# Small experts: V's blocks from the 16th on by indirect loads that leave out unpicked rows, with fewer identity products and moved row sums

## The reference, cut to what matters

```python
def peer_ffn(h, w_query, sub_keys, expert_u, expert_v):      # 256 tokens, D = 1024
    q = (xt @ w_query).reshape(T, 8, 2, 128)
    scores = einsum('thpc,hpnc->thpn', q, sub_keys)          # 8 heads, 2 x 128 keys
    ...                                                      # the 16 best key pairs of each head
    idx = ...                                                # 128 of 16384 experts for each token
    gate = softmax(best_s)
    act = gelu(einsum('cd,ced->ce', x, expert_u[idx]))
    y = einsum('ce,ced->cd', gate * act, expert_v[idx])
```

## Time and profile before

| | us |
|---|---|
| median of 3 runs | 2841.92 |
| lowest and highest run | 2835.9 and 2845.36 |
| the profiled execution, its own time | 2837.32 |
| its span | 2835.4 |
| first and last `back` of the first layer (start) | 1336.47 and 1873.93 |
| the same of the second layer | 2278.58 and 2816.04 |

### The profile page before, as it was taken

One profiled execution on the slowest core, in us unless ns is written; L12 is line 12 of the kernel. 1 busy time (PEld: TensorE's weight loads), 2 busy tenths in 40 slices (PEclk: granted clock), 3 DMA queues, 4 the chain that ended last, 5 costly groups with the idle time before them and its releaser, 6 DMA issues. The chain is left out here.

```text
span 2835.4 us, 45847 instructions
## 1 busy us (share of the span) xinstructions
PE 2671.6 (94%) x18652; PEld 2063.7 (73%) x18652; DVE 1527.5 (54%) x2976; ACT 519.8 (18%) x1030; POOL 612.9 (22%) x657
## 2 busy tenths in 40 slices
PE   8989988999987799889999999999998999999997
PEld 8978856555543687889777766678698977776665
DVE  5786533111100455789555467645467965537774
ACT  4543212000000253222000000014432200000000
POOL 0012100111110000114333344400001443325441
PEclk9999989999999899999999999999999999999999
DMA  7410029999999723689999999954258999999995
GB/s 221 151 48 3 3 104 383 419 418 420 419 420 395 263 65 108 227 293 404 409 409 409 365 409 409 409 195 150 82 190 308 364 407 409 409 370 406 409 409 204
DMA packets 260111, 843.20 MB, mean 297 GB/s; under 512 B 30258, under 2 KB 96306, under 8 KB 234944
## 3 DMA queue, kind: packets, MB, share of 16 engines
q1 hardware_dynamic: 182480, 567.60, 52.0%
q0 software_dynamic: 77424, 272.68, 24.4%
HBM read 881.07 MB, written 11.27 MB: 315 GB/s over the span
## 5 line engine op out<-in xcount | busy, mean ns | idle before, releaser
L166 PE MATMUL psum<-constants 128*128 128x256 f32 x2264 | 539.4, 383 | 21.1 <-DMA token_results<-expert_rows,place 11.2
L2418 PEld LDWEIGHTS psum<-all_gates 128*128 128x128 f32 x4096 | 482.8, 193 | 75.0 <-issue 63.0
L166 PEld LDWEIGHTS psum<-constants 128*128 128x128 f32 x2264 | 425.4, 192 | 138.9 <-issue 80.4
L2418 PE MATMUL psum<-all_gates 128*128 128x128 f32 x4096 | 489.2, 277 | 18.3 <-ACT act L2489 10.1
L2441 PE MATMUL psum<-v_raw,act 128*128 128x512 f32 x1024 | 481.4, 592 | 0.7 <-ACT act L2489 0.7
L2538 POOL DMA_INDIRECT all_gates<-expert_u_rows_dram,all_gates x256 | 255.0, 996 | 1014.5 <-DVE all_gates L2615 552.6
L2661 DVE CUSTOM_DVE_ANT_0 all_gates<-all_gates,psum 128x1024 f32<-128x1024 f32 x256 | 309.2, 1219 | 205.9 <-DMA all_gates<-expert_u_rows_dram,all_gates 203.8
L2670 DVE SCALAR_TENSOR_TENSOR psum<-all_gates,psum 128x1024 f32<-128x1024 f32 x254 | 327.1, 1288 | 145.9 <-DMA all_gates<-expert_v_dram,all_gates 141.3
L2538 POOL DMA_INDIRECT all_gates<-expert_v_dram,all_gates x256 | 253.1, 989 | 326.1 <-DVE psum L2670 197.0
L1741 PE MATMUL psum<-piece_raw,tile_cols 128*64 128x256 f32 x2496 | 287.9, 381 | 17.8 <-DMA piece_raw<-w_up_dram 7.6
L2441 PEld LDWEIGHTS psum<-v_raw,act 128*128 128x128 f32 x1024 | 194.4, 190 | 136.7 <-issue 122.4
(11 more groups left out here) (518 smaller groups left out, 3125.1 us busy)
## 6 DMA issues: line engine op xcount, KB each, us to landing
all_gates<-expert_u_dram SPq DMA_DIRECT2D x256, 512.0 KB
v_raw<-expert_v_dram SPq DMA_DIRECT2D x256, 512.0 KB
piece_raw<-w_gate_dram SPq DMA_DIRECT2D x78, 1024.0 KB, 15.0
piece_raw<-w_up_dram SPq DMA_DIRECT2D x78, 1024.0 KB, 23.4
piece_raw<-w_down_dram SPq DMA_DIRECT2D x78, 1024.0 KB, 20.1
in_raw<-w_in_dram SPq DMA_DIRECT2D x48, 1024.0 KB, 11.1
query_raw<-w_query_dram SPq DMA_DIRECT2D x16, 1024.0 KB, 6.5
w_o<-w_o_dram SPq DMA_DIRECT2D x16, 512.0 KB
```

The costliest lines, as they stand in the source:

```text
L166: nc.tensor.matmul(S["psum"][:, bank, T:].rearrange("p (i n) -> p i n", n=P), ident, ident.unsqueeze(1).to_broadcast([P, 2, P]), start=Tru ...
L2418: last = nc.tensor.matmul(PS[:, bank, 0:P], raw_u[:, n % RAW_U, c * P:(c + 1) * P], h_full[:, c, :], start=(c == 0), stop=(c == KD - 1), s ...
```

## The change

- V's blocks 16 to 127 no longer come from SP but from POOL (`load_wanted`), by indirect loads. DVE's `want` marks, in four parts of 28 blocks at the turns 0 to 3 of the back loop, each row whose gate is zero for all dense tokens; such a row gets an index beyond the bound and keeps what the buffer held. A load waits for its part's marks and for PE's `back(n - 7)`.
- POOL's picks stand in its program behind the V load of the same turn (`picks_after`), no longer in one run.
- `FILL` goes from 4 to 2. The last 56 blocks of U are spread over the first 104 turns (`dense_after`).
- Eight picks move into `select(1)` (`beside`), the last ten picks into the layer norm between its halves (`last_picks`).
- The Gelu of the row sums is taken in two halves, behind the gelu of blocks 86 and 106.

```diff
-    FILL = 4
+    SUMS_AFTER = (EARLY + 14, EARLY + 34)
+    FILL = 2
+    DENSE_SPAN = 104
+    BESIDE_CHOICE = 8
+    LAST_PICKS = 10
+    WHOLE, PARTS = 16, 4
...
+        def picks_after(n):
+            before = BESIDE_CHOICE + BESIDE_HOTS * SPREAD
+            left = 2 * PICKS - LAST_PICKS - before
+            return range(before + n * left // N, before + (n + 1) * left // N)
+
+        def dense_after(n):
+            first, last = (min(N - E, m * (N - E) // DENSE_SPAN) for m in (n, n + 1))
+            return range(E + first, E + last)
...
                 for n in range(N):
-                    if n + RAW_V < N:
+                    if n + RAW_V < WHOLE:
                         load_v(n + RAW_V)
...
                     back(n)
-                    if E + n < N:
-                        dense(E + n)
+                    for m in dense_after(n):
+                        dense(m)
                     stay_busy(nc, S, 2, FILL)
...
-                    if n == E + 50:
-                        eng.wait_ge(picked_done, PICKS)
-                        nc.scalar.activation(own_share, own_sum, ACT.Gelu).then_inc(sums_done, 1)
+                    if n in SUMS_AFTER:
+                        h = SUMS_AFTER.index(n)
+                        eng.wait_ge(picked_done, (h + 1) * PICKS // 2)
+                        nc.scalar.activation(own_share[:, half(h)], own_sum[:, half(h)], ACT.Gelu).then_inc(sums_done, 1)
...
+                def load_wanted(n):
+                    part = (n - WHOLE) * PARTS // (N - WHOLE)
+                    pool.wait_ge(wanted_known, part + 1)
+                    pool.wait_ge(y_done, n - RAW_V + 1)
+                    nc.gpsimd.indirect_dma_start(
+                        out=raw_v[:, n % RAW_V, :], out_offset=None, in_=S["v_rows"],
+                        in_offset=bass.IndirectOffsetOnAxis(ap=load_row[:, n:n + 1], axis=0),
+                        bounds_check=LAYERS * N * N - 1, oob_is_err=False).then_inc(some_in[n % RAW_V], 16)
...
+                for s in range(BESIDE_CHOICE + BESIDE_HOTS * SPREAD + RING):
+                    load_picks(s)
+                for n in range(N):
+                    if WHOLE <= n + RAW_V < N:
+                        load_wanted(n + RAW_V)
+                    for s in picks_after(n):
+                        if s + RING < 2 * PICKS:
+                            load_picks(s + RING)
...
+                def want(part):
+                    size = (N - WHOLE) // PARTS
+                    j = slice(WHOLE + part * size, WHOLE + (part + 1) * size)
+                    step(nc.vector.tensor_reduce(wanted[:, j], G[:, :, j].rearrange("p t j -> p j t"), X, ALU.max))
+                    step(ts(wanted[:, j], wanted[:, j], 0.0, float(1 << 20), ALU.is_le, ALU.mult))
+                    step(tt(wanted[:, j], wanted[:, j], block_row[:, j], ALU.add))
+                    nc.vector.tensor_copy(load_row[:, j], wanted[:, j]).then_inc(wanted_known, 1)
```

More of the change, by code:

```diff
@@ L2248, in _, with layer_norm @@
                            norm)
-def layer_norm(dve, nc, step, rows, stats, psum_halves, g, b, ready, root_ready, root_done, norm=None):
+def layer_norm(dve, nc, step, rows, stats, psum_halves, g, b, ready, root_ready, root_done, norm=None, between=None):
     for a in range(NT):
+        if a and between is not None:
+            between()
         for n in range(2):
@@ L2532, in _, with load_picks @@
             def _(pool):
-                pool.wait_ge(picks_known, 1)
-                for s in range(2 * PICKS):
+                def load_picks(s):
                     r, c = s % RING, s % PICKS
@@ L2546, in _, with pick, beside @@
                 tt, ts, stt = nc.vector.tensor_tensor, nc.vector.tensor_scalar, nc.vector.scalar_tensor_tensor
+                def pick(s):
+                    r, c = s % RING, s % PICKS
+                    dve.wait_ge(row_in[r], 16 * (s // RING + 1))
+                    row = ring[:, r, :]
+                    if s < PICKS:
+                        if s == 0:
+                            dve.wait_ge(x_copied, 2)
+                        nc.vector.tensor_tensor_reduce(row, row, both, 1.0, 0.0, ALU.mult, ALU.add,
+                                                       own_sum[:, c:c + 1]).then_inc(picked_done, 1)
+                        return
+                    dve.wait_ge(picked_done, s)
+                    if c % (PICKS // 2) == 0:
+                        h = 2 * c // PICKS
+                        dve.wait_ge(sums_done, h + 1)
+                        step(tt(own_share[:, half(h)], own_share[:, half(h)], own_gate[:, half(h)], ALU.mult))
+                    if s == PICKS:
+                        ts(both, row, own_share[:, c:c + 1], None, ALU.mult).then_inc(picked_done, 1)
+                    else:
+                        stt(both, row, own_share[:, c:c + 1], both, ALU.mult, ALU.add).then_inc(picked_done, 1)
                 def select(turn):
                     a = ORDER[turn]
+                    waiting = list(range(BESIDE_CHOICE if a == DENSE else 0))
+                    def beside():
+                        if waiting:
+                            pick(waiting.pop(0))
                     for n in range(4):
@@ L2682, in _ @@
                     gate(n)
-                before = BESIDE_HOTS * SPREAD
-                left = 2 * PICKS - before
                 for n in range(N):
@@ L2687, in _, with last_picks @@
                         gate(n + LEAD)
-                    for s in range(before + n * left // N, before + (n + 1) * left // N):
+                    for s in picks_after(n):
                         pick(s)
+                    if n in (0, 1, 2, 3):
+                        want(n)
                 dve.wait_ge(ln_in, 32)
-                dve.wait_ge(picked_done, 2 * PICKS)
+                def last_picks():
+                    for s in range(2 * PICKS - LAST_PICKS, 2 * PICKS):
+                        pick(s)
+                    dve.wait_ge(picked_done, 2 * PICKS)
                 layer_norm(dve, nc, step, S["x"], stats, lambda a, n: PS[:, 4 + 2 * a + n, :],
                            raw_u[:, 0, :], raw_u[:, 1, :], lambda a, n: dve.wait_ge(quarter_done, min(2 * a + n + 1, 2)),
-                           root_ready, root_done, norm)
+                           root_ready, root_done, norm, between=last_picks)
 def program(nc, dram, out):
```

66 lines of the change are left out of this document (39 added, 27 removed).

## The result

| | before | changed |
|---|---|---|
| median (us), runs | 2840.38 (2835.90 to 2845.36), 4 | 2813.90 (2811.86 to 2818.71), 4 |
| ratio | | 0.9909, 95% interval 0.9887 to 0.9931 |
| profiled execution, span | 2837.32, 2835.4 | 2812.25, 2810.5 |
| granted clock over the span | 0.983 | 0.957 |

A forecast was written before the change was run, and what follows sets the result against it. DMA bytes, closely followed by PE's stream, were taken to bound the back loop: 2837.3 - 179.0 (loops) + 26.8 (tail) + 1 (clock) + 6 (head) = 2692, as a median 2696 us; own range 2653 to 2725, with POOL's rival to 2755.

The forecast's parts named there:

- prediction's own signs of being wrong: Stage over 475 us in either layer, head growing by over 10 us, or clock leaving 1.00 in the back loop.
- The bound: Back loop, 537.5 us a layer: PE never waits, DMA moves 402 to 409 GB/s, "the most they do"; both limits close.
- The bytes: Back loop: 338 and 336 blocks left to load, at 409 GB/s 433 and 431 us; DMA the tighter limit.
- (b): Back loop: absent rows fall unevenly over partitions, so a DMA engine ends V's share late, at most 4 and 8 us.
- (d): Back loop: V now waits in one queue behind picks; no size of its own, within 14 us for four things.
- (a) POOL's pace: POOL's issues in the back loop: up to 9 us over DMA; as a rival, stage 473, median 2747, chance 22%.
- (c) The marks: DVE's new `want` in the back loop's first turns: 4.4 us a reduction, 20 us for four, nothing on the path.
- absent rows save nothing: Rival, back loop: partly absent loads hold their queue place as long as full ones; 488 us, median 2777, chance 6%.
- Lock step: Rival, back loop: V's loads land too late behind picks on q0; stage 554, time 2904, slower; chance 5%.
- The tail: Ten picks between the layer norm's halves, 13.4 us unhidden a layer: +26.8 for two layers, +1 for clock.
- The head: Eight picks in `select(1)` fall into DVE's waits for Exp and the lists; 3 us a layer, +6, from 0 to 20.
- The clock: Rival, back loop: gaps from less filler lower PE's clock, up to 3.5 us more each 3.54 us turn; chance 2%.

The follow-up runs named there:

- no_rows: Changed kernel with every row of V's blocks 16 to 127 counted as absent, so those loads carry nothing: 2684.3 us, ratio to before 0.9460.
- all_rows_no_marks: Changed kernel with every row of V's blocks 16 to 127 loaded and no marks computed on DVE: 2787.5 us, ratio to before 0.9822.
- four_in_flight: Changed kernel with V's indirect loads at most 4 ahead in place of 7, real absent rows and whole result kept: 2719.4 us, ratio to before 0.9589.
- all_rows: Changed kernel with every row of V's blocks 16 to 127 loaded by the same indirect loads, marks computed but zeroed: 2800.8 us, ratio to before 0.9862.
- the first experiment: The run all_rows: changed kernel with no row of V left out, marks computed but zeroed; 2800.8 us against the changed kernel's 2813.9.
- blocks_absent: Changed kernel, but 3 of every 8 of V's blocks from the 16th wholly absent, the others whole (37.5% of rows): 2702.9 us, ratio to before 0.9516.
- v_by_sp_no_head: Changed kernel with V loaded whole by SP, no marks, no picks inside the norm and none beside the choice: 2797.0 us, ratio to before 0.9853.
- sp_earlier_picks: Changed kernel with V loaded whole by SP, no marks, no picks inside the norm, loop picks done by block 104: 2841.3 us, ratio to before 0.9999.
- even_absent: Changed kernel with 37.5% of V's rows absent by partition divided by 16 plus partition modulo 8, remainder 0 to 2 by 8: 2726.4 us, ratio 0.9613.
- mod8_absent: Changed kernel with 37.5% of V's rows absent, partitions with remainder 0 to 2 by 8 in every block from the 16th: 2790.1 us, ratio 0.9827.

## Why the prediction was wrong

Two of the prediction's own signs of being wrong came: the stage is over 475 us in both layers, and the clock leaves 1.00 in the back loop.

- **The bound.** Right. Bytes and PE's stream do lie close together: no_rows has the loop at 431 against 427.6 for the stream, and with all rows (all_rows_no_marks) 484.7 and 483.5 against the 488 of 380 blocks at 409 GB/s. That 409 is "the most they do" is a misreading, though: the page of the kernel before has 418 to 420 GB/s in an earlier stage. It is what this stage's loads reach.
- **The bytes.** The count was exact, the packets show it. The step that failed is the one that divides them by an undisturbed 409 GB/s, with (b), "at most 4 and 8 us", and (d), V's place in one queue behind picks, inside the 14 us for all of (a) to (d). The mixture cost 10% of the throughput instead: 373 GB/s in the steady part. The stage was 505 and 489 in place of 448, and four_in_flight puts 47 and 35 us of that on the depth of the queue. With the queue short the loop takes 457 and 454, within 10 us of the forecast, and the whole kernel, 2719.4 us, lies in the stated range. An estimate from the Trainium skill, DMA: Bandwidth & Descriptors, section Bandwidth (341 GB/s at 1 MB), would have given a stage of 520. That is nearer to the outcome, but all_rows and four_in_flight reach 409 and 404 with blocks of half a megabyte and less, so the size of a load isn't the reason at work.
- **(a) POOL's pace.** In four_in_flight POOL issues as much, and from 1460 to 1660 us PE is busy 198.7 of 200. The rival that gave it 22% is out.
- **(c) The marks.** Sized at 4.4 us a reduction and "nothing on the path". The line's own row shows 6.3 us:

```profile
L2743 DVE TENSOR_REDUCE all_gates<-all_gates x8: 6284/6297/6308, 1347.2 to 2308.7; 128x28 f32<-128x3584 f32 x8
```

  Its input is read across the tile, at 1.76 ns an element, where the contiguous one of the earlier trace rows took 1.24; that the order of reading makes the difference wasn't tried apart. DVE was full from 1360 to 1400, and the throughput fell to 331 GB/s in 1380 to 1420. It is the marks: in the same 40 us all_rows has 366 GB/s and all_rows_no_marks 409. That they merely delay refills was the error: in a stage bound by bytes a delayed load is lost time, 13 us in all.
- **The rival "absent rows save nothing"** (6%, 2777) is what the outcome looks like, and the first experiment seemed to say so. Its mechanism, that such a load holds its place as long as a full one, comes close with the deep queue (242 loads in 300 us, where full ones are 234), but absent rows don't force it: four_in_flight serves 258 of the same loads in that time. no_rows and blocks_absent say nothing of it, since none of their loads has both kinds. It was the case to take more seriously: the trace of before had no load with mixed rows whose time could be read, and I kept that unknown at 8 us rather than bound it by a full load.
- **Lock step** (5%, 2904) had the right ingredient, the seven loads of V behind eight picks on one queue, and the wrong direction: it asked whether rows would come in time and took a deeper queue for safety.
- **The tail.** 13.85 us for ten picks, as forecast (13.4); but in the second layer the picks before them were late, 8 us more.
- **The head.** Forecast +3, measured +9.6 in the first layer. I had let eight picks fall into two waits that "end by PE's progress". The wait for Exp did shrink, from 4.70 to 0.49 us, and took 4 us of them. The wait for the lists is still 7.62 and ends 8.9 us later (1251.89 in the earlier trace rows, 1260.80 now): it ends by a chain that DVE itself starts. By v_by_sp_no_head the eight picks are worth 4.4 us of the 9.6. But each of these is a single trace, and kernels with the same work ahead of the loop begin it anywhere from 1336.5 us (no_rows) to 1348.0 (sp_earlier_picks), so neither figure is firm and the other 5 us need no cause in the change.
- **The clock.** It left 1.00 in the loop (0.66 over 1820 to 1850), where PE stood idle for more than half of the time. That is a result of the slow stage rather than its cause: four_in_flight, with the same products, has 1.00 from 1420 to 1800.

## What to carry to other kernels

Leaving rows out of indirect loads saves their bytes, but measure the throughput of loads that are partly absent before you divide by that of full ones, and try a shorter queue at once: here three loads fewer in flight were worth 94 us and cost one constant. Judge a stage by when the next one starts, not by its own last product: identity products left out saved 81 us in the loops and 41.5 in all. When bytes bound a stage, no work that delays a load's issue is hidden, and a wait that ends by a chain which the engine itself starts is no cover for work put ahead of it. Before reading "issue" or "remote" as a cause, see whether the trace has its landings.

## What was not expected of the hardware

- Indirect loads with 37 to 40% of their rows absent move 363 to 392 GB/s by the pattern, 373 for the real rows, with up to seven loads of V and eight picks in the queue; the real rows 397 with four and eight. Whole loads move 409, wholly absent ones mixed with whole ones 406.
- A load of V is 18 us old at landing with seven in flight and all rows (15.7 to 17.8 in even_absent and mod8_absent), and 9.7 with four, at nearly the same throughput (409 and 397 GB/s): the rest of the time bought almost nothing.
- With 37.5% of the rows absent the loop takes anything from 441 to 486 us, by their pattern over partitions and blocks alone, with the queue deep.
